# Hybrid trunk on one core: second-half transposes of the wide experts cut to the rows in use, and the first input block loaded by two queues

## The reference

```
h = h + W_out [ rmsnorm(DilatedAttn(q,k,v)) ; rmsnorm(S5(u)) ]     # [q|k|v|u] = rmsnorm(h) @ W_in
h = h + CrossAttn(rmsnorm(h), rmsnorm(mem))
h = h + MoE(rmsnorm(h))                                            # top 4 of 32 experts
out = rmsnorm(h)

def expert_block(xb, e):                  # w1[e] 1024 x 2048, w2[e] 1024 x 1024
    hb = xb @ w1[e] + b1[e]
    x_glu = min(hb[:, :1024], 7);  x_lin = clip(hb[:, 1024:], -7, 7)
    act = x_glu * sigmoid(1.702 * x_glu) * (x_lin + 1)
    return act @ w2[e] + b2[e]
```

## Time and profile before

| | |
|---|---|
| median of 3 runs | 2473.04 us (2470.52 to 2473.25) |
| profiled execution | 2472.86 us, span 2471.2 us |
| PE busy | 2418.2 us, 98% of the span |
| DVE, ACT, POOL busy | 711.8, 382.5, 495.3 us |
| transposes of line 2018 | 384, 51.6 us busy |
| experts | from about 791 us to the end |

### The profile page before, as it was taken

How to read it: one execution, slowest core, us unless ns; L and a number is a source line. 1 busy time by engine, 2 the same in 40 slices (tenths; PEclk the granted TensorE clock), 3 DMA queues, 4 the chain that set the end, 5 groups by cost and what they waited for, 6 DMA issues and landing times.

```text
span 2471.2 us, 35415 instructions
## 1 busy us (share of the span) xinstructions
PE 2418.2 (98%) x14592; PEld 1955.1 (79%) x14592; DVE 711.8 (29%) x1859; ACT 382.5 (15%) x846; POOL 495.3 (20%) x994
## 2 busy tenths in 40 slices
PE   9999998999997999999999999999999999999997
PEld 5455566445565899999999999999978888787875
DVE  3112287222554221222222222222222222122223
ACT  2020176112332000000010001101101001010002
POOL 4988852220011000000001100000100000000001
PEclk9999999999997999999999999999999999999999
DMA  8450110500025545466666777788998898988886
GB/s 229 111 97 35 69 53 19 189 34 35 0 111 221 206 164 197 177 227 229 234 232 232 242 255 280 255 282 297 300 342 326 318 345 301 351 320 318 318 313 261
DMA packets 242001, 526.77 MB, mean 213 GB/s; under 512 B 32029, under 2 KB 45597, under 8 KB 241836
## 3 DMA queue, kind: packets, MB, share of 16 engines
q1 hardware_dynamic: 226736, 482.44, 53.1%
q0 software_dynamic: 13968, 41.85, 7.7%
q10 hardware_dynamic: 1132, 0.16, 0.0%
HBM read 489.91 MB, written 48.24 MB: 218 GB/s over the span
## 4 chain that ended last, share of the span: by engine, by line
PE 95%; DVE 2%; issue 1%; DMA 1%; ACT 0%; POOL 0%; POOLq 0%; SPq 0%; ACTq 0%; DVEq 0%
PE ps L2038 43%; PE ps L2069 12%; PE ps L1287 11%; PE ps L637 9%; PE ps L2048 8%; PE ps L2018 2%; PE ps L939 1%; PE ps L2026 1%; PE ps L951 1%; PE ps L927 1%; PE ps L1294 1%; PE ps L619 1%; PE ps L719 1%; PE ps L2059 1%; PE ps L624 1%
## 5 line engine op out<-in xcount | busy, mean ns | idle before, releaser
L2038 PE MATMUL ps<-xT,wch 128*128 128x128 f32 (+16 forms) x8192 | 1086.7, 294 | 1.0 <-issue 1.0
L2038 PEld LDWEIGHTS ps<-xT,wch 128*128 128x128 f32 x8192 | 1068.2, 191 | 16.1 <-issue 7.2
L2125 DVE TENSOR_SCALAR glu<-ps,b1s 128x128 f32<-128x128 f32 (+16 forms) x256 | 96.2, 376 | 757.7 <-PE ps L2038 755.1
L2069 PE MATMUL ps<-act,wch 128*128 128x256 f32 (+15 forms) x2048 | 308.7, 313 | 0.0
L2069 PEld LDWEIGHTS ps<-act,wch 128*128 128x128 f32 x2048 | 303.2, 190 | 3.6
L2241 ACT ACTIVATE sg<-glu 128x256 f32<-128x256 f32 (+16 forms) x128 | 58.7, 458 | 1221.8 <-DVE glu L2125 1207.5
L1960 POOL COPY b1s<-b1T 128x16 f32 x32 | 6.3, 196 | 1023.8 <-DVE outT L2143 690.9
L2048 PE MATMUL ps<-wch,act 128*128 128x512 f32 x480 | 208.5, 592 | 0.0
L2048 PEld LDWEIGHTS ps<-wch,act 128*128 128x128 f32 x480 | 90.1, 190 | 107.6 <-issue 107.6
L1969 POOL DMA_INDIRECT acc_dram<-orow,idx_s x47 | 74.7, 1590 | 455.6 <-ACT orow L2225 239.7
L637 PE MATMUL ps<-xnT,wa 128*128 128x512 f32 x384 | 165.6, 592 | 0.0
(11 more groups left out here) (338 smaller groups left out, 2029.4 us busy)
## 6 DMA issues: line engine op xcount, KB each, us to landing
wch<-in_w SPq DMA_DIRECT2D x128, 2048.0 KB, 12.1
wch<-in_w SPq DMA_DIRECT2D x128, 1024.0 KB, 8.9
b2bc<-in_b SPq DMA_DIRECT2D x16, 512.0 KB, 14.0
wa<-in_w_in SPq DMA_DIRECT2D x3, 2048.0 KB, 10.7
acc_dram<-h SPq DMA_DIRECT2D x10, 512.0 KB, 2.9
skew_dram<-line_dram SPq DMA_DIRECT2D x8, 576.0 KB, 11.9
xrow<-in_x SPq DMA_DIRECT2D x8, 512.0 KB, 8.0
wa<-in_w_xkv SPq DMA_DIRECT2D x2, 2048.0 KB, 7.8
```

Source lines behind the costliest of these rows:

```text
L2038: last = nc.tensor.matmul(m.ps[:, 2 + g % 3, part * WIN:part * WIN + W], m.wch[2 * h + part][:, k, cols], m.xT[i % 2][:, k, 0:W], start=(k ...
L2069: last = nc.tensor.matmul(m.ps[:, 5 + j % 3, 0:W], m.wch[4 + k // 2][:, k % 2, j * P:(j + 1) * P], m.act[i % 2][:, k, 0:W], start=(k == 0) ...
L2125: v.tensor_scalar(m.glu[:, b, n, 0:W], bank[:, 0:W], m.b1s[:, i % 2, j:j + 1], LIMIT, ALU.add, ALU.min).then_inc(glu_ok, 1)
```

## The change

There are two edits. In `transposes_in`, the transposes of a half read only the rows that the width holds: `rows = min(P, WIDE[i] - P * half)`. For half 0, for expert 0 and for the narrow experts that is 128 as before; for the second half of experts 1 to 15 it is 100 down to 8. The stationary operand is then `xg` with that many rows, the moving operand the identity's first rows x rows. In `phase_ab`, the first block of x is loaded as two halves of 512 columns, one by SP's queue, one by ACT's queue ahead of its three loads; both add 16 to `x_in[0]`, and its two waiters wait for 32.

```diff
     def sync(sp):
-        sp.dma_start(m.xrow[:, 0], a.x[0:P]).then_inc(x_in[0], 16)
+        sp.dma_start(m.xrow[:, 0, 0:512], a.x[0:P, 0:512]).then_inc(x_in[0], 16)
         for b in range(1, NB):
...
     def scalar(act):
+        act.dma_start(m.xrow[:, 0, 512:D], a.x[0:P, 512:D]).then_inc(x_in[0], 16)
         act.dma_start(m.g_mix[:], a.norm_mix.rearrange("(k p) -> p k", p=P)).then_inc(mix_in, 16)
...
         def square(b):
-            act.wait_ge(x_in[b], 16)
+            act.wait_ge(x_in[b], 16 if b else 32)
...
         def rows(lo, hi):
             for b in range(lo, hi):
-                pe.wait_ge(x_in[b], 16)
+                pe.wait_ge(x_in[b], 16 if b else 32)
...
                     for half in range(halves(i)):
-                        at = width * n + P * half
-                        last = nc.tensor.transpose(m.ps[:, q % 2, at:at + P], m.xg[i % 2][half][:, k * P:(k + 1) * P], m.ident[:])
+                        at, rows = width * n + P * half, min(P, WIDE[i] - P * half)
+                        last = nc.tensor.transpose(m.ps[:, q % 2, at:at + rows], m.xg[i % 2][half][0:rows, k * P:(k + 1) * P], m.ident[0:rows, 0:rows])
                 last.then_inc(x_full, 1)
```

## The result

The changed kernel took 2500.78 us in the median of 4 executions (2492.72 to 2502.26), against 2472.39 (2470.52 to 2473.25) before: ratio 1.011, 95% interval 1.0097 to 1.0122. The profiled execution was the shortest of the four, 2492.72 us with a span of 2491.1, 19.9 us above the one of before. So the forecast of 2494 us had the right side, the right size for the profiled execution, and was 3 to 7 us short of the medians. The runs show what the 21 us are. For the rest they show a cause in one trace, and that it holds for the other executions is inferred.

The account below looks back on a forecast made before the run. PE was taken as the bound, busy 98% of the span. Mode changes in 12 experts add 21.9 us, three experts save 0.8, the first block 0: 2472.9 + 21.1 = 2494.0 us, range 2485 to 2502.

Parts of the forecast that it names:

- The price of the transposes: Experts' transpose groups: mode changes stop PE and expose loads, 21.9 us more in 12 experts, 0.8 less in three.
- the bared load of a product: First product behind a mode change: its two-pass load is no longer hidden, 0.105 us on top of the 0.093 us stop.
- Which halves change mode: Second halves of experts 1 to 15: 58 to 8 rows change mode (12 experts); 100, 96 and 68 don't.
- The faster one: Rival: no price for alternating, cut transposes cost the larger of streaming and 0.062 us; 2466.5 to 2467.6 us, chance 0.05.
- Only the stop, the load hidden: Rival: each mode change in a group costs only 0.093 us, 1.428 us a group; 2485.4 us, chance 0.05.
- All 15 change the mode: Rival: the three experts with 100, 96 and 68 rows change mode too, 6.6 us more; 2501.4 us, chance 0.04.
- The clock within the experts: Rival: the clock falls to 0.50 after one transpose group in four, 11 us more; 2505 us, chance 0.03.
- the step on the first block: Start of the kernel: splitting block 0's load is neutral, taken as 0, since bytes ahead of block 1 stay the same.
- that slack: Start: DVE's first copy with the gain is needed by PE's fifth turn at 9.4, leaving some 2.9 us.
- My bound of -1.15 to +1 us: Start: the split load gains at most PE's 1.15 us idle before block 1, or loses up to 1 us.

Follow-up runs that it names:

- the reordered run: Transposes' edit without the split load, each group's four transposes of half 0 before half 1's four: 2475.76 us, ratio 1.0016 against the kernel before.
- 64 against 68: Transposes' edit without the split load, second halves under 65 rows given 64 rows: 2496.41 us; second halves under 68 given 68 rows: 2469.16 us.
- the run with 68 rows: Transposes' edit without the split load, every second half given at least 68 rows: 2469.16 us, ratio 0.9987 against the kernel before.
- the split alone: Kernel before with only the first block's load split over two queues, transposes unchanged; measured twice: 2477.74 us and 2476.37 us.
- the second trace: The changed kernel measured once more with no edit: 2496.97 us, ratio 1.010 against the kernel before; its profiled execution took 2499.8 us.
- the 22.1 of the transposes: Kernel before with the transposes' edit alone, input loaded as before: 2494.2 us, ratio 1.0086, +22.1 us.
- the late gain's run: Kernel before, nothing split, the gain's load issued last on ACT's queue behind `ohb` and `rb`: 2484.26 us, ratio 1.0043.

## Why the prediction was right, and what it missed

**The price of the transposes was right**, term by term. A change of mode holds PE and exposes the next load: the groups came out at 1.88 us for 1.87 with 58 rows, and 1.50 + 0.20 = 1.70 for 1.71 with 8 rows. The experts cost 21.47 us where 21.1 was summed. One reading is slightly off: 0.54 - 0.429 is 0.11 us for the bared load of a product, not 0.105, which makes 0.1 us in 24 groups. That the cause is the change and not the size is shown by the reordered run (same transposes, +2.46 us), that the price hangs on whether more than 64 rows are left by 64 against 68 (+24.0 against a gain). The edit cuts the moving operand's columns with the rows; that these alone don't stop PE can be read in the kernel before:

```profile
692.46 1.88 PE L1287 MATMUL ps<-wd,oT 128*128 128x512 f32 x4
694.18 1.87 PE L1287 MATMUL ps<-wrg,hmT 128*128 128x32 f32 x16
```

Four products 512 wide, then the first of 32, all with 128 rows: 1.72 us for four is 0.43 each, the undisturbed spacing. What the runs don't separate is the stop from the bared load; only their sum is measured.

**Which halves change mode** was right too: 68, 96 and 100 rows stay with the full array. The group for 100 rows took 0.80 us and its products 0.02 more than before (6.93 for 6.91 in the first fence on the experts' ends and the earlier trace rows), 0.82 in all where 0.78 was given.

**The rivals.** The faster one has its price (0.06 us for a cut transpose) right and its condition wrong: it holds in the run with 68 rows. "Only the stop, the load hidden" is refuted by every group, 1.88 and 1.70 us where it had 1.43. "All 15 change the mode" is refuted by the groups of 100, 96 and 68 rows, which got shorter. The clock within the experts is refuted too: it is 1.00 from 800 us on in both traces.

**What failed** is the step on the first block, in its sentence on the gain: "with 1.47 / 2 = 0.73 for the copy some 2.9 us of slack". I set the 0.47 us of later issue against that slack. The load landed 7.3 and 8.9 us after its issue where it had taken 4.8 (5.7 and 6.9 in the two traces of the split alone), so in the changed kernel it came 2.9 and 4.5 us later, once past the slack. I also counted PE's start on the second block as fixed at 7.67; in the second trace that block came early, and PE was ready for the fifth turn at 8.1 in place of 9.4. And I left the clock out of it: the fifth turn started at 11.00, 1.6 us later than before, yet the products started 4.9 us later. The other 3.3 us were lost behind the pause, where the clock was at 0.50. The split costs 5.7 and 4.5 us in the medians of its two measurements; with the 22.1 of the transposes that makes 26.6 to 27.8, against 24.8 and 28.4 measured for both. My bound of -1.15 to +1 us for this edit was too narrow by 3.5 to 4.7 us; that the total stayed inside the range is luck in so far as the room was left for other rivals. So is the near hit on the profiled execution: in it the gain came just in time, and the clock's earlier rise ahead of the experts took 1.6 us back.

**Left open.** Why the gain's load takes longer behind half a block (other packets of ACT's queue, or the input blocks of SP's) wasn't separated, nor why the second block came early in some traces. No trace of the split alone fell on one of its longer times; their cause is inferred from the second trace of the changed kernel and from the late gain's run.

## What to carry to other kernels

Before cutting rows off a stationary operand, look at what stands beside it: each change between an operand of 128 rows and one of 64 or fewer cost about 0.15 us ahead of a transpose and 0.2 ahead of a product, while a full transpose costs 0.109 us in all. Operands of 68 to 100 rows beside full ones cost nothing (65 to 67 rows weren't run). Stay at 68 or more, or put equal shapes together, and end on the instruction whose length covers the next load. A small load that everyone waits for belongs at the head of its queue; half a block ahead of it brought the first block forward by 0.1 us and cost 4.5 to 5.7 in the median.

## What the runs showed of the hardware that was not expected

- A float32 transpose with 68 stationary rows let the next follow after 0.06 us although both loads are 128 columns wide, while the products behind such a group came 0.05 us late, so that the two-pass load of a product needs about 0.11 (0.06 + 0.05): groups of 0.69 us, then 5.36 for 5.31.
- A 4 KB load in single elements landed 4.8 and 4.2 us after its issue at the head of ACT's queue, 5.7, 6.9, 7.3 and 8.9 behind half a block, and 13.6 behind the 148.5 KB table and the bias table. Half a block (256 KB) took 3.2 us at the head of that queue and 6.5 behind the 4 KB of the gain.
- Fifteen second halves, three prices: 58 to 8 rows beside full ones 1.69 to 1.50 us a group, 68 rows 0.69, 100 rows 0.80, for 0.875 with all full.
- A pause of 2.90 us at 8 to 11 us was followed by 10 us at the 1.2 GHz level, though PE worked through all of them and in another execution was granted 1.00 over the same stretch.
